# Copying the token rows of each block to the four partition groups by DMA instead of by TensorE and ScalarE, in a decoder step on one core

## The reference

```
q = h @ w_pq ; s1, s2 = q . sub_keys1, q . sub_keys2     # 8 heads, 128 keys each
16 best of each, 16 best of their sums -> expert e, gate g = softmax   # 8 x 16 = 128 experts a token
u, v = peer_u[e], peer_v[e]                                # 1024 floats each
a = gelu(h . u)
y = LN2(ALPHA * h + sum over experts of (g * a) * v + sigmoid(h @ w_ple_gate) * (p @ w_ple))
```

## Time and profile before

| | |
|---|---|
| median of 3 runs | 2129.21 us (2123.03 to 2132.95) |
| profiled execution | 2123.03 us, span 2121.0 us |
| mean granted TensorE clock | 0.833 |
| busy: PE, DVE, ACT, POOL | 1553.8, 1345.2, 690.4, 747.0 us |
| moved by DMA | 693.19 MB, of it 604.02 MB by the gathers |

### The profile page before, as it was taken

How to read it: one execution, slowest core, us unless ns; L and a number is a source line. 1 busy time by engine, 2 the same in 40 slices (tenths; PEclk the granted TensorE clock), 3 DMA queues, 4 the chain that set the end, 5 groups by cost and what they waited for, 6 DMA issues and landing times.

```text
span 2121.0 us, 22969 instructions
## 1 busy us (share of the span) xinstructions
PE 1553.8 (73%) x7124; PEld 790.0 (37%) x7124; DVE 1345.2 (63%) x3180; ACT 690.4 (33%) x2472; POOL 747.0 (35%) x784
## 2 busy tenths in 40 slices
PE   8988889999976676776666785557668657567654
PEld 6567675465443343333333432122222212122111
DVE  2329982235778888878888876764544454544544
ACT  0012222220334443444444442333333333223322
POOL 0001115300144454435444445454343444444432
PEclk9988989999988888888877887668878878779877
DMA  7010017973499999989999989999997999999997
GB/s 302 1 53 1 1 51 289 372 267 155 159 379 410 400 406 408 399 349 416 411 413 393 409 357 401 405 389 399 419 373 317 398 421 416 418 388 393 422 421 292
DMA packets 99094, 693.19 MB, mean 327 GB/s; under 512 B 10800, under 2 KB 15664, under 8 KB 21936
## 3 DMA queue, kind: packets, MB, share of 16 engines
q0 software_dynamic: 82944, 604.02, 69.9%
q1 hardware_dynamic: 16048, 87.89, 10.6%
HBM read 687.00 MB, written 4.87 MB: 326 GB/s over the span
## 4 chain that ended last, share of the span: by engine, by line
PE 41%; DMA 25%; DVE 19%; issue 7%; ACT 4%; POOL 3%; POOLq 0%; ACTq 0%; DVEq 0%; SPq 0%
DMA R<-d_uv,E 25%; PE bank L914 13%; DVE R L1660 7%; PE bank L593 5%; PE bank L705 4%; PE bank L808 3%; PE bank L864 3%; POOL R L554 3%; PE bank L845 3%; PE bank L891 2%; PE bank L587 2%; PE bank L642 1%; DVE E L1599 1%; DVE E L1596 1%; ACT E L1213 1%
## 5 line engine op out<-in xcount | busy, mean ns | idle before, releaser
L914 PE MATMUL bank<-R,E 128*32 128x512 f32 x2304 | 731.4, 806 | 506.2 <-ACT E L1218 506.2
L554 POOL DMA_INDIRECT R<-d_uv,E x576 | 677.6, 1176 | 1029.9 <-PE bank L914 577.2
L1660 DVE CUSTOM_DVE_ANT_0 R<-R,E 128x1024 f32<-128x1024 f32 x576 | 692.0, 1224 | 419.3 <-DMA R<-d_uv,E 405.1
L914 PEld LDWEIGHTS bank<-R,E 128*32 128x32 f32 x2304 | 234.4, 133 | 956.6 <-ACT E L1218 702.7
L1210 ACT ACTIVATE E<-E 128x2 f32<-128x2 f32 x288 | 57.9, 201 | 341.9 <-DVE E L1660 341.4
L1218 ACT ACTIVATE E<-E 128x32 f32<-128x32 f32 x576 | 153.6, 313 | 9.4
L864 PEld LDWEIGHTS bank<-E,W 128*128 128x128 f32 x1280 | 144.4, 192 | 18.2 <-issue 16.8
L864 PE MATMUL bank<-E,W 128*128 128x128 f32 (+1 forms) x1280 | 148.0, 276 | 1.1 <-ACT E L1121 1.1
L1213 ACT ACTIVATE E<-E 128x1 f32<-128x1 f32 x576 | 138.2, 287 | 12.4
L1161 ACT CAST E<-E 128x4 uint32<-128x4 f32 (+1 forms) x146 | 27.7, 191 | 341.6 <-DVE E L1660 341.6
L593 PE MATMUL bank<-E,W 128*128 128x288 f32 x384 | 95.9, 414 | 9.4 <-DMA E<-d_xT 9.4
(11 more groups left out here) (280 smaller groups left out, 1717.3 us busy)
## 6 DMA issues: line engine op xcount, KB each, us to landing
R<-d_kc SPq DMA_DIRECT2D x8, 2560.0 KB, 12.6
R<-d_vc SPq DMA_DIRECT2D x8, 2560.0 KB, 9.6
R<-d_uv,E POOLq DMA_INDIRECT x576, 10.3
W<-d_w_pq SPq DMA_DIRECT2D x4, 2048.0 KB, 16.3
W<-d_w_in SPq DMA_DIRECT2D x3, 2048.0 KB, 15.8
R<-d_w_out SPq DMA_DIRECT2D x2, 2048.0 KB, 8.1
W<-d_w_gate SPq DMA_DIRECT2D x2, 2048.0 KB, 15.6
E<-d_xT SPq DMA_DIRECT2D x2, 1152.0 KB, 9.1
```

What stands on the lines that cost most here:

```text
L554: pool.indirect_dma_start(ring[r], None, A["uv"], bass.IndirectOffsetOnAxis(ap=stage[:, half, s:s + 1], axis=0),).then_inc(landed[r], 16)
L914: last = mm(acc[p0:p0 + TG, half * 512:half * 512 + 512], wsel[:, r, :], ring[r][:, D + half * 512:D + half * 512 + 512], start=False, sto ...
L1660: last = nc.vector.tensor_tensor_reduce(ring[r][:, 0:D], ring[r][:, 0:D], hrep[:, js[s], :], 1.0, 0.0, ALU.mult, ALU.add, dots[:, x, s:s + 1])
```

## The change

`hrep` is filled by DMAs from SBUF to SBUF. Each copies 32 rows of `hS` (32 partitions x 4 KB, 128 KB) to one of four groups of 32 partitions of `hrep[:, j]`: 16 for a block. For block 0 SP issues all 16, behind its last load of `w_pq`, once `out_full` is 5 and the first block of `h` is ready. For the later blocks ScalarE issues them, 8 behind half-turn 30 and 8 behind half-turn 31, at the places where its copies stood; for the fifth block only the first 8. TensorE's 72 matmul instructions of line 891 and ScalarE's 36 copies of line 1191 are gone, and line 904 no longer waits for `hrep`. VectorE waits for the DMAs' semaphores at half-turns 0 and 1 of a block. `fold` shrinks from [128, 128] to [128, 32], gets a tensor of its own and is loaded at the start of the program instead of at 465 us.

```diff
-            load(fold, A["fold"], in_fold)
...
+            sp.wait_ge(out_full, BLOCKS)
+            sp.wait_ge(h_ready, 1)
+            for j in range(SG):
+                for s in range(SG):
+                    load(hrep[TG * s:TG * s + TG, j, :], hS[TG * j:TG * j + TG, 0, :], in_hrep[j // 2])
...
-            def spread_h(b, x):
-
-                pe.wait_ge(h_ready, b + 1)
...
-                for n in range(4 * x, 4 * x + 4):
-                    j, half = divmod(n, 2)
-                    if n >= 2:
-                        pe.wait_ge(hrep_ready, spread_count(b) + n - 1)
-                    mm(bank[:, 4 + 2 * (b % 2) + half, :], fold[TG * j:TG * j + TG, :],
-                       hS[TG * j:TG * j + TG, b, half * 512:half * 512 + 512], start=True, stop=True).then_inc(
-                           spread_full, 1)
...
                 if h0 * HALF == b * EXP:
-                    pe.wait_ge(hrep_ready, spread_count(b + 1))
+                    if b >= 2:
+                        pe.wait_ge(acc_used, b - 1)
...
-                for n in range(4 * x, 4 * x + 4):
-                    j, half = divmod(n, 2)
-                    act.wait_ge(spread_full, spread_count(b) + n + 1)
-                    nc.scalar.copy(hrep[:, j, half * 512:half * 512 + 512],
-                                   bank[:, 4 + 2 * (b % 2) + half, :]).then_inc(hrep_ready, 1)
+                act.wait_ge(h_ready, b + 1)
+                for j in range(2 * x, 2 * x + 2):
+                    for s in range(SG):
+                        act.dma_start(hrep[TG * s:TG * s + TG, j, :],
+                                      hS[TG * j:TG * j + TG, b, :]).then_inc(in_hrep[x], 16)
...
-                        dve.wait_ge(hrep_ready, spread_count(b) + 4 * (js[0] // 2) + 4)
+                        dve.wait_ge(in_hrep[js[0] // 2], 16 * 2 * SG * (b + 1))
```

More of the change, by code:

```diff
@@ L76, in token_groups @@
     return list(range(SG))
[L79 to L86, removed]
 def turns(engine, h0, h1, half_turn):
@@ L224, in build @@
         ident = sb("ident", [P, P])
+        fold = sb("fold", [P, TG])
         iota = sb("iota", [P, PK])
@@ L275, in build @@
         keep = view(E, 17444, D)
-        fold = view(E, 19296, P)
         keysT = view(E, 19040, 2, NKEY)
@@ L336, in build @@
         in_out = [sem(f"in_out{i}") for i in range(2)]
-        in_gate, in_rows2, in_keys, in_fold = sem("in_gate"), sem("in_rows2"), sem("in_keys"), sem("in_fold")
+        in_gate, in_rows2, in_keys = sem("in_gate"), sem("in_rows2"), sem("in_keys")
         in_pq = [sem(f"in_pq{i}") for i in range(4)]
@@ L368, in build @@
         gx_ready, gexp_done, picked, laid = (sem(n) for n in ("gx_ready", "gexp_done", "picked", "laid"))
-        spread_full, hrep_ready = sem("spread_full"), sem("hrep_ready")
+        in_hrep = [sem("in_hrep0"), sem("in_hrep1")]
         staged, granted, slot_free, dotted, gelued, weighed, diagonal = (
@@ L401, in _ @@
             load(ident[:, :], A["ident"], in_const)
+            load(fold[:, :], A["fold"], in_const)
             load(iota[:, :], A["iota"], in_const)
@@ L664, in _ @@
             pe.wait_ge(u_done, CT)
-            pe.wait_ge(in_const, 16 * 2)
+            pe.wait_ge(in_const, 16 * 3)
             pe.wait_ge(in_Bt, 16)
@@ L919, in experts @@
                 turns(pe, h0, h1, half_turn)
-                for x in range(2):
-                    if b < QB and spreads(b + 1, x) and h1 * HALF == (b + 1) * EXP - HALF * (1 - x):
-                        spread_h(b + 1, x)
             pe.wait_ge(at_done, QB)
@@ L953, in _ @@
             pe.wait_ge(out_used, BLOCKS)
-            for x in range(2):
-                spread_h(0, x)
             pe.wait_ge(h_ready, BLOCKS)
@@ L1184, in spread_h @@
             def spread_h(b, x):
-                if b == 0:
-                    act.wait_ge(in_fold, 16)
-                for n in range(4 * x, 4 * x + 4):
-                    j, half = divmod(n, 2)
-                    act.wait_ge(spread_full, spread_count(b) + n + 1)
-                    nc.scalar.copy(hrep[:, j, half * 512:half * 512 + 512],
-                                   bank[:, 4 + 2 * (b % 2) + half, :]).then_inc(hrep_ready, 1)
+                act.wait_ge(h_ready, b + 1)
[3 more added lines that the diff above has]
+                                      hS[TG * j:TG * j + TG, b, :]).then_inc(in_hrep[x], 16)
             def experts(h0, h1):
@@ L1217, in half_turn @@
                         for s in range(g * PAIR, g * PAIR + PAIR):
-                            f(wsel[:, x * HALF + s, :], fold[:, 0:TG], ACT.Copy,
+                            f(wsel[:, x * HALF + s, :], fold[:, :], ACT.Copy,
                               scale=wts[:, x, s:s + 1]).then_inc(diagonal, 1)
                 turns(act, h0, h1, half_turn)
-                for x in range(2):
-                    if b < QB and spreads(b + 1, x) and h1 * HALF == (b + 1) * EXP - HALF * (1 - x):
+                for x in range(2 if b + 1 < QB else 1):
+                    if b < QB and h1 * HALF == (b + 1) * EXP - HALF * (1 - x):
                         spread_h(b + 1, x)
@@ L1809, in layouts @@
     a["ident"] = np.eye(P, dtype=np.float32)
-    a["fold"] = np.tile(np.eye(TG, dtype=np.float32), (SG, SG))
+    a["fold"] = np.tile(np.eye(TG, dtype=np.float32), (SG, 1))
     a["iota"] = spread(np.arange(PK, dtype=np.float32))
```

## The result

The changed kernel takes 2154.87 us, median of 6 runs (2148.9 to 2159.12); the kernel before took 2127.65 beside it (6 runs). The ratio is 1.0118, with a 95% interval of 1.0099 to 1.0137: slower by about 27 us, and just past the 2154 at which the predicted range ended. The profiled execution took 2152.67 us.

What follows compares the result with a forecast made beforehand. From 560 us on, the DMA engines bound the kernel: bytes at 407 GB/s plus gather starvation. Copies 43.9, less 2 and 34.6, plus 1 of gaps gave +8.3 us on 2129.2, so 2137 us; range 2118 to 2154.

Steps and rivals of the forecast that it cites:

- 43.9 (copies): Added copies on the DMA engines: 9.4 MB at 215 GB/s, sized from 64-partition transfers, 9.75 us a block.
- 2 (idle engines at the start): Start of the experts: about 2 us of block 0's copying lie on idle DMA engines before the first gather.
- 34.6 (starvation): Start and first three switches: time lost against 407 GB/s while gathers starve, 34.6 us, the most the removal could win.
- 1 (gaps left): Start and switches: the copies' own load closes all remaining DMA gaps but 1 us.
- The engines count as busy for the slow half too, so it isn't left to the gathers: Copies on the DMA engines: at half rate their whole time counts as cost, 9.75 us a block.
- I work with the larger: Start and first three switches: takes starvation by rate, 34.6 us, over that by DMA share, 28.5 us.
- By place: Net change at start, first, second, third and fourth switch: +0.7, +2.1, +2.1, -2.4, +4.9 us.
- The issues: DMA issues: 0.49 us each, eight holding ScalarE 3.9 us (up to 11.3); SP's 16 take 7.9 us.
- Late landing: First three switches: copies queue beside gathers, VectorE waits, 12 us more; +20 us, 2149 us; chance 0.19.
- Full rate: Copies run at the gathers' 407 GB/s: with gaps left -3 us, 2126 (chance 0.21); without, 2116 (chance 0.10).
- full rate and no gaps left: Copies at full rate with all starvation ended: 21 - 34.6 = -13 us, 2116 us; chance 0.10.
- A quarter of the rate: Copies at 107 GB/s because reading and writing the same half of partitions halves the rate again: +51 us, 2180; chance 0.05.

Runs made afterwards that it cites:

- a1_no_copies: The changed kernel without the copies for blocks 1 to 4, which use block 0's rows; 2112.46 us, ratio 0.9919 to the kernel before.
- p7_step4: The kernel before plus 96 extra 128 KB copies in blocks 0 and 1, each written to 32 partitions lying 4 apart; 2153.50 us, ratio 1.0100.
- a2_sp_issues: The changed kernel with SyncE instead of ScalarE issuing the 56 copies of blocks 1 to 4; 2157.34 us, ratio 1.0153 to the kernel before.
- a3_step4: The changed kernel with all 72 copies writing partitions 4 apart, so rows stand in wrong places; 2120.04 us, ratio 0.9937 to the kernel before.

## Why the prediction failed

The forecast was 43.9 (copies) - 2 (idle engines at the start) - 34.6 (starvation) + 1 (gaps left) = +8.3 us. Measured: +27.2. The bound was read rightly, and that the copies run far below the full rate and fill the gaps. The term for the copies was mis-sized, and that is shown; the term for the starvation may have been, and that is not.

**The step that failed: "At 215 GB/s a block costs 9.75 us, all 43.9 us", with "The engines count as busy for the slow half too, so it isn't left to the gathers".** Measured, the packets of the changed kernel add up to 56.3 us: +12.4. Bursts of 8 alone say 0.81 us a copy where the forecast had 0.61, so 72 x 0.81 = 58 us, and no compute engine is seen to wait for those. The two parts of the 56.3 show where the step went wrong. The copies' own packets take 35.4 us, 0.49 a copy, less than forecast. The other 20.9 us are packets of the gathers that became longer, and the forecast had put those at nothing. The rows that I sized it from are transfers with 64 partitions that ran with nothing beside them. Running alone, such a transfer shows its own packets only; no row of the kernel before could show what it adds to gathers beside it.

**"I work with the larger", 34.6 us of starvation.** The DMA share gave 28.5, the rate gave 34.6. By the share the sum is 6.1 us higher, and 8.3 + 12.4 + 6.1 = 26.8 us, against 27.2. That so near a sum comes out is in part luck, for the experiments don't settle the term: `a1_no_copies` leaves 19 to 35 us, with a share of 0.94 still in one window. And both numbers were read from one execution, the quickest of its round. The window over the start reads 0.87 and 335 GB/s in it, but 0.74 to 0.83 and 282 to 318 GB/s in the nine other profiles whose code is the same at that place (part of this is a first gather up to 3.6 us later). The lowest of them, `p7_step4`:

```profile
560.00:600.00 40.00, 37.41 (x172) 22.36 (x171) 24.37 (x61) 12.29 (x34) 12.74 (x12) 0.79 0.74 282
```

The two pages are no second proof of the sum. Packets added less idle time filled is the difference of two spans whatever the cause; here it is 56.3 us of packets for a span 29.9 us longer, so about 26 us of idle time were filled.

**By place.** Forecast +0.7, +2.1, +2.1, -2.4, +4.9; measured +3.9, +6.7, about +7, -1 to +1, +8.5. Each is 1.4 to 5 us worse, the fourth switch, where only the cost stands, by 3.6. The fourth is the dearest and the third the cheapest, as forecast.

**The issues** took 4.46 to 5.47 us for seven in a row on ScalarE, 0.64 to 0.78 each and not 0.49, inside the bound of 1.41, and SP's 16 took 10.55 and not 7.9. They cost nothing that shows: with all of them on SyncE the time is the same. Two smaller steps failed beside this one: at the start VectorE did not find groups 0 and 1 landed but waited 6.51 us, and at the third switch its two waits of 8 us were not gone but became 4.95 and 3.78.

**Late landing**, the rival that gave 2149, the nearest to the truth in time. Its mechanism is there: VectorE waits for the copies three times, 16.2 us in all, at most 6.5. But little of the 27 us can be its. Bursts of copies that no engine but SyncE is seen to wait for cost 0.81 us each, about as much as the copies of the changed kernel (0.76 to 0.83), and in `a2_sp_issues` VectorE waits only 10.3 us for them with no gain in time. A few us of it are not ruled out, at the fourth switch above all, where eight copies cost 8.5 us and VectorE waits 5.89.

**Full rate**, the two rivals below: refuted for 32 neighbouring partitions. With the partitions spread, `a3_step4` lies at -13.2, where "full rate and no gaps left" had put -13; that the numbers agree so well is luck in part, since that sum uses the 34.6 us too.

**A quarter of the rate** (+51): no. The whole cost by the packets, 0.82 us for 128 KB, is 160 GB/s, between half and a quarter of the gathers' 407.

The Trainium skill ("SBUF — State Buffer", section "Door 1: the DMA port swizzle") holds that 32 neighbouring partitions reach only 8 of the 16 ports. The experiments agree that which partitions are touched decides (32 spread over 128 cost 20.2 us where 32 neighbours cost 62.4). They show it for the written side alone: 32 partitions read cost 14.4. The page's 189 GB/s for a transfer by itself would have put the sum 6 us higher, +14, still short of +27; it too leaves out what the transfer does to the ones beside it.

What stays open: how much of the starvation could be won, and by what path a narrow write lengthens the gathers' packets; the records give times of packets, not what they stood for. A layout of the slots in which the four groups are interleaved over the partitions would let `a3_step4` compute the right rows at the same copies; this was not tried, nor was one DMA that writes all 128 partitions from 32.

## What to carry to other kernels

Where the DMA engines are the bound, a transfer moved onto them costs its packets and what it adds to the others' packets. Judge it by a transfer with the same written partitions beside the same traffic, not by one that ran alone, and spread its destination over all partitions if the layout allows. Read starvation from more than one profiled execution, for it differed here from one to the next by several us at one place. And before moving work off an engine look for a dependent step that merely stands in its way: here moving one step of the order gave 8.8 us, where the new transfers lost 27.

## What the runs showed of the hardware that I had not expected

- SBUF writes to 32 neighbouring partitions cost 62 to 77 us for 12.6 MB beside gathers; to 32 partitions 4 apart 20.2; over 128 partitions 16.5; HBM writes from 32 partitions 14.4.
- The gathers' packets, all 604.02 MB of them to 128 partitions, took 21 us more DMA time beside 72 narrow copies and 26 to 32 us more beside 96; beside 24 wide copies, or 96 written 4 apart, none more.
- With a DMA share of 1.00 and 407 GB/s in the middle of a block, 12.6 MB of wide copies still fitted in for 16.5 us (11 to 22 by the interval of the ratio), at 414 GB/s in all: a share of 1.00 there was not the last of the rate.
